# A ring of gathered expert rows with seven places in place of nine, in a two-layer hybrid attention and PEER kernel

## What is computed

```
def block(xb):                                   # 128 tokens
    q = (xb @ wq).reshape(tb, 8, 2, half)
    s1, s2 = q[:, :, 0] @ sub_k1.T, q[:, :, 1] @ sub_k2.T
    v1, i1 = lax.top_k(s1, 16); v2, i2 = lax.top_k(s2, 16)
    ...
    top_s, pos = lax.top_k(cand_s, 16)           # of 256 sums, per head
    eid = take_along_axis(cand_i, pos).reshape(tb, 128)
    gate = softmax(top_s).reshape(tb, 128)
    a = einsum("td,tkd->tk", xb, expert_u[eid])
    w = gelu(a) * gate
    return einsum("tk,tkd->td", w, expert_v[eid])
```

## Time and profile before

| what | value |
|---|---|
| median of 3 runs | 4599.48 us (4595.16 to 4602.47) |
| profiled execution, span | 4597.2 us |
| PE busy | 3084.2 us (67%) |
| DVE busy | 3112.0 us (68%) |
| POOL busy | 1510.9 us (33%) |
| ACT busy | 906.1 us (20%) |
| moved by DMA | 1517.96 MB, 1347.13 of them on the queue of the gathers |
| granted clock, mean | 0.830 |

### The profile page before, as it was taken

The page is one execution under the profiler, slowest core; times in us unless marked ns, Lnnn a source line. Parts: engine busy times, 40 slices in busy tenths (PEclk is TensorE's granted clock), DMA queues, the critical chain, the costliest instruction groups (busy, mean ns, idle before and its releaser), DMA issues.

```text
span 4597.2 us, 49199 instructions
## 1 busy us (share of the span) xinstructions
PE 3084.2 (67%) x16384; PEld 1197.3 (26%) x16384; DVE 3112.0 (68%) x8352; ACT 906.1 (20%) x2464; POOL 1510.9 (33%) x1378
## 2 busy tenths in 40 slices
PE   8889996757885455554665786778885555545554
PEld 4445444312231111111221222555331111111111
DVE  2352337878778778777878764634687877877886
ACT  2442212111111111111111111541121111111211
POOL 0000113444443444444434332010344444444443
PEclk9989999878997777777887898997996777787767
DMA  4342228999999999999999996121999999999998
GB/s 157 123 165 92 78 78 323 415 414 400 418 418 396 414 417 408 418 415 403 387 419 395 414 400 232 35 97 69 359 408 400 408 419 415 405 419 411 397 418 348
DMA packets 307838, 1517.96 MB, mean 330 GB/s; under 512 B 26272, under 2 KB 94368, under 8 KB 143744
## 3 DMA queue, kind: packets, MB, share of 16 engines
q0 software_dynamic: 185888, 1347.13, 71.3%
q1 hardware_dynamic: 87616, 133.07, 8.4%
q10 hardware_dynamic: 34080, 34.62, 2.2%
HBM read 1498.51 MB, written 16.20 MB: 329 GB/s over the span
## 4 chain that ended last, share of the span: by engine, by line
DVE 40%; PE 28%; DMA 19%; issue 7%; ACT 4%; POOL 1%; DVEq 1%; ACTq 0%; POOLq 0%; SPq 0%
DMA X<-in_uv_dram,X 17%; DVE X L2041 16%; PE ps L1121 7%; PE ps L580 6%; DVE X L2052 2%; ACT X L1572 2%; PE ps L1038 1%; DVE X L1942 1%; DVE X L1940 1%; DVE X L1943 1%; DVE X L2048 1%; PE ps L1104 1%; PE ps L915 1%; PE ps L803 1%; POOL X L2175 1%
## 5 line engine op out<-in xcount | busy, mean ns | idle before, releaser
L1121 PE MATMUL ps<-X 64*64 64x512 f32 x2560 | 1628.7, 769 | 1269.7 <-DVE X L2052 1256.1
L2175 POOL DMA_INDIRECT X<-in_uv_dram,X x1280 | 1429.8, 1117 | 2168.8 <-PE ps L1124 1698.7
L2041 DVE CUSTOM_DVE_ANT_0 X<-yT,X 128x1024 f32<-128x1024 f32 x1280 | 1531.1, 1223 | 319.3 <-DMA X<-in_uv_dram,X 269.9
L1122 PE MATMUL ps<-X 64*64 64x512 f32 x2560 | 1628.8, 770 | 0.0
L1124 PE MATMUL ps<-X 64*64 64x512 f32 x2560 | 1628.8, 770 | 0.0
L1123 PE MATMUL ps<-X 64*64 64x512 f32 x2560 | 1628.8, 770 | 0.0
L1121 PEld LDWEIGHTS ps<-X 64*64 64x64 f32 x2560 | 358.3, 162 | 2442.9 <-DVE X L2052 1746.0
L1572 ACT ACTIVATE X<-X 128x1 f32<-128x1 f32 x1280 | 256.5, 202 | 2279.4 <-DVE X L2041 2214.7
L1124 PEld LDWEIGHTS ps<-X 64*64 64x64 f32 x2560 | 358.5, 162 | 0.0
L1122 PEld LDWEIGHTS ps<-X 64*64 64x64 f32 x2560 | 358.4, 162 | 0.0
L1123 PEld LDWEIGHTS ps<-X 64*64 64x64 f32 x2560 | 358.4, 162 | 0.0
(11 more groups left out here) (293 smaller groups left out, 3569.8 us busy)
## 6 DMA issues: line engine op xcount, KB each, us to landing
wring<-in_ada_w_dram SPq DMA_DIRECT2D x48, 1024.0 KB
wring<-in_w_in_dram SPq DMA_DIRECT2D x36, 1024.0 KB
wring<-in_peer_wq_dram SPq DMA_DIRECT2D x24, 1024.0 KB
X<-in_uv_dram,X POOLq DMA_INDIRECT x1280
wring<-in_w_out_dram SPq DMA_DIRECT2D x8, 1024.0 KB
X<-scores ACTq DMA_DIRECT2D x64, 128.0 KB
X<-mods ACTq DMA_DIRECT2D x15, 512.0 KB, 8.5
ahead<-X ACTq DMA_DIRECT2D x18, 256.0 KB
```

The lines of the kernel that those rows point to most:

```text
L1121: pe.matmul(ps[0:HD, h, :], dg(slice(0, HD), s), v0[0:HD], **ends)
L1122: pe.matmul(ps[HD:P, 2 + h, :], dg(slice(HD, P), s), v0[HD:P], **ends)
L2041: v.tensor_tensor_reduce(uvr[:, slot, 0:D], h2[:, t, :], uvr[:, slot, 0:D], 1.0, 0.0, ALU.mult, ALU.add, adot[:, s_:s_ + 1]).then_inc(S("d ...
L2175: g.indirect_dma_start(uvr[:, slot, :], None, a["uv"], bass.IndirectOffsetOnAxis(ap=istages[i % 2][:, s:s + 1], axis=0)).then_inc(S(f"uv{s ...
```

## The change

One constant. The ring keeps seven places; the 16 KB of each partition that the other two held are not used for anything else. Seven is odd like nine, so two gathers are still released by one pair: gathers 7 and 8 counted from an even slot n wait for the pair of slots n and n + 1. No engine's instructions change in number or order; what changes is the value that POOL waits for, and the place and semaphore of a slot.

```diff
-UVRING = 9
+UVRING = 7
```

## The result

Seven places take 4854.14 us (median of 4 runs, 4849.95 to 4856.25) where nine take 4599.42: ratio 1.055, 95% interval 1.0538 to 1.0563. The forecast was 4827 in a range of 4760 to 4911. The profiled execution has a span of 4852.1 us, 254.9 more than before.

The account below looks back on a forecast made before the run. It took a loop through the nine-place ring, as long as the 41.00 us clean round, with the DMA transfers just beneath, as the bound; 151 + 76 = 227 us on the profiled 4597.2, plus 2.3, gave 4827 us, range 4760 to 4911.

Parts of the forecast that it names:

- The bound before: Clean tiles, nine places: loop from pair 0's first dot through gather 9 takes 41.00 us, sixteen gathers 39.8; both limits together.
- the 7.51 us from issue to dot: Loop leg from gather 9's issue (1984.42) to its dot (1991.93), said to contain little waiting.
- Price of a clean round: Eight pairs in a tile with only expert work and next selection: 41.00 us becomes 44.77, 3.77 more.
- The 19.76: Last loop leg: DVE finds all rows landed and its own work leads to the next round, 19.76 us.
- the three steps of 2.49: Loop leg of three further landings, up to pair 5's second dot, 7.47 us in all.
- The forty clean rounds: Rounds of the five clean tiles (2 and 3 of layer 0, last three of layer 1): 3.77 each, 151 us.
- The other forty rounds: Tiles 0, 1, 4, 5 of layer 0 and first of layer 1: 1.9 each, between 0.4 and 3.77; 76 us.
- No second hole: Gather 13, pair 6's second dot, released by pair 3: rows land with some 2.5 us left, costed at nothing.
- Not slower: Rival: the queue in front of gather 9 hides both landings; time stays 4600 us; chance 0.04.
- A much shorter leg: Rival: issue-to-dot leg shrinks once nothing is queued; halfway (5.2) the round is 43.0, total 4720 us; chance 0.10.
- Full price: Rival: 7.51 is fixed latency, landings stay ragged; clean rounds pay 5, others 2.8; 4911 us; chance 0.15.
- The signs: Changed profile: DVE's row wait about 500 us, clean tiles about 358, DMA share near 0.92, engines empty 3 to 4 us each round.

Follow-up runs that it names:

- The pieces with nine places: Nine places, next tile's selection cut into five pieces after pairs 1, 2, 4, 5 and 7 instead of three after 5, 6 and 7: 4590.07 us, ratio 0.9982.

## Why the prediction was right, point by point

*The bound before.* I wrote that the loop with nine places is already as long as the round and that both limits lie together. The first half was read too strongly: the 7.51 us from issue to dot held waiting behind other transfers. With the legs that the kernel after shows (5.9 and 3.8, medians over clean rounds), nine places give 7.79 + 5.9 + 3.8 + 2.5 + 19.9 = 39.9, about 1 us under the 40.8 that the transfers take. Of the 7.51 then 1.6 were waiting, and the median leg with nine places is 8.1. The same sum gives 42.4 with eight places (measured 42.4) and 44.9 with seven (44.8). The pieces with nine places show the same from the other side.

*Price of a clean round.* Forecast 44.77, measured 44.8. Two of its terms were wrong and cancelled: the leg from issue to dot was taken at 6.94 from one row, and is 5.9; the next landing was taken 2.81 later, and comes 3.8 later. Together 9.75 forecast, 9.7 measured: that the round came to 0.1 us was luck in these two. The 19.76 and the three steps of 2.49 came as they stood.

*The forty clean rounds* were put at 151 us and took 167. Of the 16 us that were missing 4 lie in the first rounds of the tiles, which I counted as clean ones: with 47.0 to 48.5 us, against 42.9 to 43.7, they pay 3.9 to 5.5. The other 12 lie in the rest, which grew by 4.2 in the mean (40.8 to 45.0) and not by 3.77: the one round that I took for the base, 41.00, was 0.2 longer than the mean, and some rounds after are longer than the forecast's 44.77.

*The other forty rounds* were put at 76 us, the middle between two rows, and took 86. Tile 1, which I had named as the one that grows least, grew by 18.4; the last two tiles of layer 0 grew by 17.0 and 17.5, and the first tile of layer 1 least, by 13.1. In tile 1 the queue was much as I read it: over its eight rounds the leg from issue to dot fell from 11.2 to 6.5 us in the mean, by 4.7 where 4.57 was forecast. What failed there is the price of the two landings. From the first dot that a release brings (gather 9 before, gather 7 after) to the second dot of pair 5 it took 5.2 us with nine places and takes 12.3 with seven, so the two cost 7.1 us and not 4.98. That leaves 2.4 a round, where I had 0.4; the middle of 1.9 came near the measured 2.15 for the forty rounds all the same.

*No second hole.* Right with seven places: after the four steps no dot waits for rows in 33 of the 35 clean rounds that are not a tile's first (the other two are the last of the kernel, which have no selection between their pairs). But the margin of 2.5 us was misjudged, and the term came to nothing by little. In the round shown gather 13 goes out at 3866.42, lands 9.9 us later, at 3876.3, and its dot starts at 3876.67 (POOL's timeline; issue to landing, in us; DVE's timeline):

```profile
3866.42 0.94 POOL L2175 DMA_INDIRECT X<-in_uv_dram,X  x1 [4.32 <-PE ps L1124]
X<-in_uv_dram,X POOLq DMA_INDIRECT x1, 9.9
3876.67 1.22 DVE L2041 CUSTOM_DVE_ANT_0 X<-yT,X 128x1024 f32<-128x1024 f32 x1
```

That is a margin of 0.36 us by the trace's landing time, and so it is in the median clean round. I had given this gather the 6.94 of an empty queue, but three others are still ahead of it when it is issued. With six places the hole opens at pair 6, where the margin was named.

*The rivals.* Not slower: the windows at 3852 to 3856 show the queue empty. A much shorter leg: 5.9 us was below every row I had (6.49 the least), a part of the way to it, but the second landing gave that back. By the Trainium skill ("DMA: Bandwidth & Descriptors", Anatomy of one DMA, SWDGE path) 1 MiB comes to an estimate of 4.4 us; the trace does not agree, with 5.8 from POOL's start to the landing on empty engines (5.9 to the dot). Full price, 4911, was not paid: 4.0 us a clean round in the median, not 5.

*The signs.* The DMA share of 0.92 and the hole of 3 to 4 us came as named. DVE's wait for gathered rows, put at about 500 us, is 578.4, and the clean tiles, put at 358, take 362 to 364 (the kernel's last one aside).

## What to carry to other kernels

A ring is deep enough when the slowest cycle through it, from a consumer's release over issue, transfer, use and the next release, is shorter than the time that bounds the work anyway; a DMA share of 1.0 does not show how near that is, the length of the queue at the moment of the longest pause does. Read that cycle off one period and count how many landings stand in it: each place less adds one landing, which costs nothing until the cycle passes the other bound, and more than a landing once a second cycle opens (here with six places). A burst on the consumer costs ring places: here cutting a 7.2 us block into pieces paid for one place (8 KB of each partition) in full and took back 175 of the 255 us, about two thirds, of what two places cost.

## What the runs showed of the hardware that was not expected

After the engines have run dry, two gathers that are issued 1.5 us apart do not land 2.5 us apart: the first is used 5.9 us after its issue began, the second 3.8 us after the first (medians over clean rounds, with seven, eight and six places alike), and only then the spacing is 2.49. In the round shown the window at 3856 has a share of 0.90 for 164 GB/s, where the one at 3851 has 0.94 for 378: the first packets after the hole take more than twice as long as later ones. What makes them slow was not tried. In two of 80 rounds with seven places POOL issued gather 7 not 0.84 but 3.4 us after PE's last product of pair 0; why was not tried.
